# A fourth sum unit in every block of the up projections, and two splits of g moved, in a float32 decoder trunk

## The reference

```python
D_MODEL = 2048; SEQ = 256; D_FF = 5632

def swiglu(hn, w_in, w_out):
    u = hn @ w_in                                            # 256 x 2048 by 2048 x 11264
    return (jax.nn.silu(u[..., :D_FF]) * u[..., D_FF:]) @ w_out

for layer in range(DEPTH):
    ...
    h = h + swiglu(rmsnorm(h, norm_ffn[layer]), ffn_w_in[layer], ffn_w_out[layer])
```

## Time and profile before

| | |
|---|---|
| time, median of 3 runs | 2024.52 us (2024.37 to 2027.17) |
| the profiled execution | 2024.81 us, of which the span of the trace is 2023.0 us |
| TensorE busy | 1983.0 us, 98% |
| VectorE busy | 1621.5 us, 80% |
| ScalarE busy | 1129.3 us, 56% |
| HBM traffic | 186 GB/s over the span |
| granted TensorE clock, mean | 0.998 |

### The profile page before, as it was taken

How to read it: one execution, slowest core, us unless ns; L and a number is a source line. 1 busy time by engine, 2 the same in 40 slices (tenths; PEclk the granted TensorE clock), 3 DMA queues, 4 the chain that set the end, 5 groups by cost and what they waited for, 6 DMA issues and landing times. The chain is left out here.

```text
span 2023.0 us, 26260 instructions
## 1 busy us (share of the span) xinstructions
PE 1983.0 (98%) x9919; PEld 1688.9 (83%) x9919; DVE 1621.5 (80%) x1805; ACT 1129.3 (56%) x1336; POOL 87.8 (4%) x113
## 2 busy tenths in 40 slices
PE   7999999999999999999999999999999999989999
PEld 7999988888888887888897888788888888878887
DVE  6868555789888898889876885559888888889896
ACT  5478435555555555556575664455555555556563
POOL 1030200000000000000002320000000000000000
PEclk9999999999999999999999999999999999999999
DMA  7454653555555555565555335355555555545554
GB/s 274 167 189 161 231 190 105 200 195 205 189 203 192 205 193 191 177 208 190 206 190 177 124 124 175 117 187 187 204 192 205 193 201 192 202 168 206 194 202 166
DMA packets 167679, 378.21 MB, mean 187 GB/s; under 512 B 6154, under 2 KB 10516, under 8 KB 167220
## 3 DMA queue, kind: packets, MB, share of 16 engines
q1 hardware_dynamic: 167152, 376.02, 54.3%
q0 software_dynamic: 272, 1.13, 0.2%
q10 hardware_dynamic: 180, 0.05, 0.0%
HBM read 375.08 MB, written 2.10 MB: 186 GB/s over the span
## 5 line engine op out<-in xcount | busy, mean ns | idle before, releaser
L549 ACT ACTIVATE w_hi<-raw 128x2048 fp32r<-128x2048 f32 (+2 forms) x275 | 517.3, 1884 | 371.2 <-DMA raw<-in_ffn_w_in 116.0
L1766 PE MATMUL bank<-w_hi,act_hi 128*128 128x512 f32 x1608 | 629.7, 392 | 13.9 <-DVE act_lo L1033 7.3
L1766 PE MATMUL bank<-w_hi,act_lo 128*128 128x512 f32 x1608 | 626.7, 390 | 0.0
L1766 PE MATMUL bank<-raw_lo,act_hi 128*128 128x512 f32 x1608 | 625.9, 389 | 0.0
L997 DVE TENSOR_TENSOR raw_lo<-raw,w_hi 128x2048 fp32r<-128x2048 f32 x180 | 411.7, 2289 | 145.2 <-ACT w_hi L549 143.1
L1766 PEld LDWEIGHTS bank<-w_hi,act_hi 128*128 128x128 f32 x1608 | 301.9, 188 | 79.5 <-DVE act_lo L1033 9.3
L1766 PEld LDWEIGHTS bank<-w_hi,act_lo 128*128 128x128 f32 x1608 | 301.9, 188 | 63.3
L1766 PEld LDWEIGHTS bank<-raw_lo,act_hi 128*128 128x128 f32 x1608 | 302.1, 188 | 61.8
L997 DVE TENSOR_TENSOR w_lo<-raw,w_hi 128x2048 fp32r<-128x2048 f32 (+2 forms) x95 | 208.8, 2209 | 91.4 <-ACT w_hi L549 91.1
L1057 DVE TENSOR_TENSOR raw_lo<-raw,w_hi 128x2048 fp32r<-128x2048 f32 x84 | 191.8, 2284 | 0.0
L1698 PE MATMUL bank<-w_hi,act_hi 128*128 128x512 f32 (+2 forms) x480 | 180.9, 377 | 3.1 <-DVE act_lo L1002 1.2
(11 more groups left out here) (230 smaller groups left out, 2529.6 us busy)
## 6 DMA issues: line engine op xcount, KB each, us to landing
raw<-in_ffn_w_in SPq DMA_DIRECT2D x176, 1024.0 KB, 5.2
raw<-in_ffn_w_out SPq DMA_DIRECT2D x88, 1024.0 KB, 4.9
raw<-in_lru_w_in SPq DMA_DIRECT2D x32, 1024.0 KB, 5.3
raw<-in_lru_w_out SPq DMA_DIRECT2D x16, 1024.0 KB, 5.1
raw<-in_w_o SPq DMA_DIRECT2D x16, 1024.0 KB, 5.1
raw<-in_w_ukv SPq DMA_DIRECT2D x8, 1024.0 KB, 5.3
raw<-in_w_uq SPq DMA_DIRECT2D x8, 768.0 KB, 4.5
raw<-in_w_dkv SPq DMA_DIRECT2D x8, 576.0 KB, 3.9
```

The costliest lines, as they stand in the source:

```text
L549: A.activation(flat_chunk(w_hi, s, size), flat_chunk(raw, s, size), ACT.Copy).then_inc(w_hi_done, 1)
L1766: i = T.matmul(bank[:, :], x_part, w_part, start=first and n == 0, stop=last and n == 2)
```

## The change

Blocks 1 to 10 of both up projections use sums in units 2, 3, 5 and 6 in place of 2, 4 and 6. The places of the extra tiles go in turn (units 2 and 5 place 0, units 3 and 6 place 1), so the preparation of units 5 and 6 waits for unit u - 3 to be finished instead of u - 4. There are four sets of side operands; the fourth (unit 3's) is kept in halves of three act tiles that sum units don't read (`SPARE`) and in a small new tile, and is split at step 7 of block 0. The first two of the four additions in `sums` become one instruction. Groups 0 and 1 of g are split at steps 3 and 4 of the last up block.

```diff
-S_UNITS = (2, 4, 6)
+S_ODD, S_EVEN = (2, 3, 5, 6), (2, 3, 5, 6)
+E_ODD, E_EVEN = (0, 1, 0, 1), (0, 1, 0, 1)
+SIDE_UNITS = (2, 5, 6, 3)
+SPARE = (4, 10, 12)
...
+        s_more = sb("s_more", [P, 2, P], F32R)
...
+        def place_wait(odd, u):
+            return 2 if len(units_of(odd)) == 4 and u in (5, 6) else 3
+        def side_operand(u, r):
+            j = SIDE_UNITS.index(u)
+            if j < 3:
+                return s_hi[:, j, r, :], s_lo[:, j, r, :]
+            if r < 3:
+                return act_hi[:, SPARE[r], P:SEQ], act_lo[:, SPARE[r], P:SEQ]
+            return s_more[:, 0, :], s_more[:, 1, :]
...
 (ScalarE, act_tiles)
-                    if kind in (0, 2) and b and q == 1:
+                    if kind in (0, 2) and q % 2 and k // 2 in SIDE_UNITS:
                         for n in range(2):
-                            i = A.activation(side_a[:, b - 1, n, :], hT_psum(kind, b, n), ACT.Copy,
+                            i = A.activation(side_a[:, SIDE_UNITS.index(k // 2), n, :], hT_psum(kind, b, q - 1 + n),
...
 (ScalarE, two_pass)
                     if n == 0:
                         gT_out(FB - 1, FB * (f + 1), ps[0:2])
-                        stationary(d, 1, act_slot(1))
...
 (ScalarE, up, body)
+                        if u in (3, 4) and isinstance(i, int) and i == FB - 1:
+                            stationary(d + 1, u - 3, act_slot(u - 3))
                         if u == 6:
...
-                            if isinstance(i, int) and i == FB - 1:
-                                stationary(d + 1, 0, act_slot(0))
...
 (ScalarE, up, block 0, step 7, after silu)
+                        for r in range(4):
+                            k = A.activation(side_operand(SIDE_UNITS[3], r)[0], side[:, 3, r, :], ACT.Copy)
+                        k.then_inc(side_hi, 1)
...
 (VectorE, act_tiles)
-                        elif b and q == 0:
-                            dve.wait_ge(side_copied, 3 * (kind // 2) + b)
+                        elif k // 2 in SIDE_UNITS:
+                            dve.wait_ge(side_copied, 4 * (kind // 2) + sorted(SIDE_UNITS).index(k // 2) + 1)
...
 (VectorE, sums)
-                dve.wait_ge(chunk_used, 4 * m + s - 3)
+                dve.wait_ge(chunk_used, 4 * m + s - before)
-                V.tensor_tensor(t13[:, 0, :], b11, b12, ALU.add)
-                V.tensor_tensor(t13[:, 1, :], b12, b22, ALU.add).then_inc(t_sum, 1)
+                V.tensor_tensor(t13, raw[s][:, 0:n12 + 1:n12, :], raw[s][:, n12:n22 + 1:n22 - n12, :],
+                                ALU.add).then_inc(t_sum, 1)
...
 (VectorE, two_pass)
-                    if n == 0:
-                        stationary(1, act_slot(1), DOWN_G0[d] + 2)
...
 (VectorE, up, body)
+                        if u in (3, 4) and isinstance(i, int) and i == FB - 1:
+                            stationary(u - 3, act_slot(u - 3), DOWN_G0[d + 1] + u - 2)
                         if u == 6:
                             shared_add(shared, i + (SUM_BLOCKS * f - 1), i + (FB + 2) * f)
-                            following(i, 5)
+                            following(i, 5, odd, j)
                             if isinstance(i, int) and i == FB - 1:
-                                stationary(0, act_slot(0), DOWN_G0[d + 1] + 1)
-                                down_sums(f, S_UNITS[0])
+                                down_sums(f, DOWN_SUMS[0])
...
 (VectorE, up, block 0, step 7)
+                        dve.wait_ge(side_hi, 2 * f + 2)
+                        for r in range(4):
+                            hi, lo = side_operand(SIDE_UNITS[3], r)
+                            k = V.tensor_tensor(lo, side[:, 3, r, :], hi.bitcast(F32), ALU.subtract)
+                        k.then_inc(side_lo, 1)
...
 (TensorE, up, body)
-                        if u in S_UNITS:
-                            e = sum_unit(u % 4, u % 4 // 2, S_UNITS.index(u), 2 * u, result, shared,
+                        if u in units:
+                            e = sum_unit(u % 4, place(odd, u), [side_operand(u, r) for r in range(4)], 2 * u, result,
```

More of the change, by code:

```diff
@@ L501, in flat_chunk, with units_of, unit_no, place @@
             return buf[s].rearrange("p k n -> p (k n)")[:, 0:size]
[L503 to L509, removed]
+        def units_of(odd):
+            return S_ODD if odd else S_EVEN
+        def unit_no(f, j, odd, u):
+            return (len(S_ODD) + len(S_EVEN)) * j + (SUMS * f + (0 if odd else len(S_ODD)) + units_of(odd).index(u))
+        def place(odd, u):
+            return (E_ODD if odd else E_EVEN)[units_of(odd).index(u)]
+        def place_wait(odd, u):
[7 more added lines that the diff above has]
+            return s_more[:, 0, :], s_more[:, 1, :]
         def down_sum(n):
@@ L683, in silu, with following, body @@
                     return A.activation(gtmp[:, t, :], src, ACT.Silu, scale=stat(RS + 2 * (d + 1) + t))
-                def following(i, u):
-                    i, u = i + u // 4, (u + 4) % 8
+                def following(i, u, odd, j):
+                    if u >= 4:
+                        i, odd, j = i + 1, not odd, j + (0 if odd else 1)
+                    u = (u + 4) % 8
                     if isinstance(i, int) and i == FB:
                         down_split(f, u)
-                    elif is_sum(i, u):
-                        split_sums(2 * i + ((c0 + u) // 4), u % 4, unit_no(f, i, u), u % 4 // 2)
+                    elif not (isinstance(i, int) and i == 0) and u in units_of(odd):
+                        split_sums(2 * i + ((c0 + u) // 4), u % 4, unit_no(f, j, odd, u), place(odd, u),
+                                   before=place_wait(odd, u))
                     else:
                         split(2 * i + ((c0 + u) // 4), u % 4)
-                def body(i, odd):
+                def body(j, odd):
                     result, shared = banks_of(odd)
+                    i = 2 * j + (1 if odd else 2)
                     for u in range(8):
@@ L719, in up @@
                         act.wait_ge(side_done, f + 1)
-                        A.activation(s_hi, side, ACT.Copy).then_inc(side_hi, 1)
+                        A.activation(s_hi, side[:, 0:3, :, :], ACT.Copy).then_inc(side_hi, 1)
                     if u == 7:
@@ L1206, in following @@
                         down_split(f, u)
[L1207 to L1210, removed]
+                    elif not (isinstance(i, int) and i == 0) and u in units_of(odd):
+                        if u != 2:
+                            sums(m, s, unit_no(f, j, odd, u), place(odd, u), before=place_wait(odd, u))
+                        split_sums(m, s, unit_no(f, j, odd, u), place(odd, u))
                     else:
@@ L1791, in last_unit, with down_operands, sum_unit @@
                 return i
-            def sum_unit(s, e, j, k0, result, shared, first, last, gT_needed, tiles=UP_TILES):
+            def down_operands(j):
+                return ((s_hi[:, j, r, :], s_lo[:, j, r, :]) for r in range(4))
+            def sum_unit(s, e, side_of, k0, result, shared, first, last, gT_needed, tiles=UP_TILES):
                 own = [tuple(buf[s][:, n, :] for buf in (w_hi, raw_lo)) for n in tiles]
                 t1, t3, t4 = ((sum_hi_tiles(e)[:, n, :], sum_tiles(w_lo_t, e)[:, n, :]) for n in range(3))
-                s1, s2, s3, s4 = ((s_hi[:, j, r, :], s_lo[:, j, r, :]) for r in range(4))
+                s1, s2, s3, s4 = side_of
                 b11, b21, t2, b22 = own
@@ L1809, in up, with body @@
             def up(f, c0, d):
-                def body(i, odd):
+                def body(j, odd):
                     result, shared = banks_of(odd)
+                    i, units = 2 * j + (1 if odd else 2), units_of(odd)
                     for u in range(8):
```

81 lines of the change are left out of this document (44 added, 37 removed).

## The result

The changed kernel takes 2034.45 us (median of 6 runs, 2031.43 to 2034.71) against 2025.57 for the kernel before in the same runs: ratio 1.0041, 95% interval 1.0031 to 1.0052, so 8.9 us slower. The forecast was 2030.0, 5.5 slower. The profiled spans differ by 2032.9 - 2023.0 = 9.9 us. All loads are the same, TensorE executes 60 matmuls fewer and is busy for as long as before: a matmul's own 0.39 us outlasts the spacing by 0.16, so that much of every wait counts as busy. VectorE has gained 80 us of work.

A forecast was written before the change was run, and what follows sets the result against it. TensorE bounds the up loop, VectorE close behind; after the change VectorE's loop sets the pace. Per FFN 0.55 + 2.2 + 9 x 0.57 - 5.1 = +2.8, twice +5.5: 2024.5 + 5.5 = 2030.0 us, range 2018 to 2040.

The forecast's parts named there:

- the likeliest case by itself: Whole kernel: the predictor's own case, forecast 2030.0 us, taken as 2027 to 2033 us; chance 0.45.
- the loop is longer: Rival, up blocks: merged addition no cheaper than two, or unit 2's data 0.2 late; 2034 to 2040 us; chance 0.17.
- the start of the up projection: Two more ScalarE copies there delay VectorE's third and fourth act_lo tile: +0.55 us per FFN.
- The forecast's loop: Up blocks: VectorE's work from shared addition to unit 6's split, then unit 6 on TensorE, sets 42.98 us a block.
- TensorE's wait before unit 3: Each up block: TensorE is free before unit 3's split is ready and waits about 0.9 us.
- ScalarE's copy of g: Up blocks, unit 2: transposed g comes at most 0.2 us late, swallowed by the wait before unit 3.
- The fast rival: Up blocks: VectorE's loop is shorter than summed, TensorE stays the bound; at 41.73 us a block, 2008 us; chance 0.12.
- waits that cost nothing: Up blocks: VectorE's waits for its own results are free in the new order, loop 1.4 us shorter; chance 0.02.
- The first block: First block after block 0: unit 3's sums and g come late; unit 7 starts 2.2 us later per FFN.
- such a fall: Up blocks: clock drops to 1.2 GHz after waits; every block 2060 us, chance 0.06; first block only 2033 us, chance 0.15.
- The move: Transition to down projection: splitting groups 0 and 1 of g earlier removes an act_lo wait and slow matmuls: gain 5.1 us per FFN.
- the 1.5 us wait: TensorE's wait on leaving the up loop, said to stay.

The follow-up runs named there:

- 9: Changed kernel with eight small extra VectorE additions nobody waits for, right before unit 2's sums: 2047.57 us.
- 10: Changed kernel with eight small extra VectorE additions nobody waits for, between unit 6's split and unit 7's: 2035.78 us.
- 3: Changed kernel with four sum units in odd blocks and three (2, 5, 6) in even ones: 2026.41 us, ratio 1.0001 to the kernel before.
- 5: Changed kernel with unit 5's second addition of the sums cut from 512 columns to 8 (t2 wrong there): 2030.60 us.
- Experiment 4: Kernel before with only the start's two extra 128x256 ScalarE copies, VectorE's tiles 6 and 7 waiting for them: 2027.32 us, ratio 1.0013.
- 7: Changed kernel with ScalarE doing a quarter's high parts and side copies before the next quarter's squares, ahead of each up projection: 2026.96 us.
- experiment 1: Kernel before, three sum units, with only groups 0 and 1 of g split at steps 3 and 4 of the last up block: 2013.34 us.
- 2: Changed kernel with groups 0 and 1 of g split at their old places: 2046.67 us, ratio 1.0104 to the kernel before.
- 6: Changed kernel with the second addition of the sums cut to 8 columns in units 3, 5 and 6 (t2 wrong there): 2025.10 us.

## Why the prediction was right or wrong

**The number: inside the range, partly by luck.** 2034.45 us lies in 2018 to 2040 but 4.4 above the forecast and above the likeliest case by itself, 2027 to 2033. It falls where the rival "the loop is longer" was priced, and neither of that rival's reasons came: the merged addition was cheaper than the two, and VectorE never waited for unit 2's data. The direction rests on the loop, which is shown; the size of the total was missed mainly by one term, the start of the up projection.

**The pace of the blocks: right, and shown.** The forecast's loop gives 42.98, measured 43.08; the sums took 2.59 for 2.58 four times over, and the rest is small change of a few hundredths at several places. 0.1 us in 18 blocks is 1.8 us; one block of FFN 1 took 43.5 (VectorE waited 0.51 before unit 1's split there, for ScalarE's high part). Experiments 9 and 10 show that it is this order and not VectorE's load, 3 that it is a matter of one block, 5 that the way goes past unit 3. TensorE's wait before unit 3 is 0.64 by the profile, about 0.8 from start to start, for 0.9 forecast, and before unit 6 it is 0.1 for 0.2. ScalarE's copy of g costs it some hundredths there, where the forecast had at most 0.2. The fast rival, a shorter VectorE loop, fell; so did waits that cost nothing: the spacing of an addition whose result the next one waits for is 0.72 in the changed kernel too (545.03 to 545.75), against 0.61 where the next doesn't wait (545.75 to 546.36).

**Unseen: a second loop**, through unit 3 and four units on TensorE, 0.3 below the first. It changes nothing of the result, but the forecast's fast rival priced blocks of 41.73 for a VectorE loop 1.25 shorter; with cuts behind unit 3 they would, by this sum, have stopped at 42.75.

**The first block: right** (+2.2 forecast, +2.1 and +2.3). The four small subtractions took the 0.8 that I had put (380.96 to 381.77), and TensorE waited 1.4 there for ScalarE's copy of g and then 0.6 for unit 3's split, where the forecast had 2.6 for the two.

**The start of the up projection: the mis-sized term.** Its 0.55 counted the delay only; measured 2.2 and 2.4. The pause grew to 2.5 us, and with it the clock fell (0.83 over 10 us). The forecast had priced such a fall for the first block's wait and for every block, and not at the one place where a pause of 1.7 was there to grow. In FFN 0 the delay itself was 0.73, and 1.45 more go with the fall. Experiment 4 shows that the copies alone do it, 7 that the fall goes with the pause. This is 3.5 of the 5.8 us by which the terms' 11.3 exceed the forecast's 5.5; the blocks bring the other 2.3. Outside the terms some 1.3 us come back, which leaves the 9.9 of the spans. In the timed runs it may be less: experiment 4 leaves that open, while experiment 7 speaks for most of it.

**The move: right in its sum, wrong in its parts.** -5.1 forecast, -5.0 and -5.2 measured. The forecast said that the 1.5 us wait would stay, and gave no reason; it was for group 0, and went (experiment 1). Against this, two waits at the transition were larger than foreseen: 0.9 before the transposes of g, of which the forecast said nothing (they wait for the gate, L1227, which the late shared addition pushes; no run tests this alone), and 0.7 before down unit 2 instead of 0.4.

**The clock in the blocks: right.** It stays at 1.00 behind waits of 0.6 us a block and behind the 1.4 and 0.6 of the first.

## What to carry to other kernels

When one engine's work is traded for another's, compare not the two loads but the longest closed way through both queues, from a wait back to the same wait; here 41.8 us of VectorE work (43.08 less 1.3 of idle time) and 41.73 of TensorE's (42.41 less 0.68 for three matmuls) made a block of 43.1. Then look for the next way just below it, before pricing a cure. A pause that is near the length behind which the clock was seen to fall isn't priced by its growth alone, and a wait put down to "issue" should be read against what each other engine ended just before. The cheapest 12 us in this kernel were two splits moved a little ahead, and such a wait was part of them.

## What the runs showed of the hardware that was not expected

A pause of 1.75 us at the start of the up projection left the clock at 1.00; pauses of 2.4 to 2.5 us at the same place came with 1.2 GHz for the next 2.7 us of matmuls (granted clock 0.83 over 10 us) in the profiled executions of the changed kernel and of experiments 2 to 6, 9 and 10. Each of these pauses, the short one too, stands right behind eight 128x128 transposes (1.04 us); whether these matter, no run tests. The clock falls near the pause's end and not at its start: in the changed kernel it is 1.00 until 322.60 and 0.78 over 322.60 to 323.35, where TensorE starts again; in the second FFN it is 1.00 until 1315.30, where TensorE starts, and 0.79 over the 1.7 us behind it. A VectorE addition of 25 columns costs 0.1 us from start to start when nobody waits, one of 8 columns that is waited for 0.20.
